# The first recurrence of a fused block, computed two heads at a time

## The reference, cut to what matters

```python
# q, k, v: [heads=4, tokens=512, 64];  g = cumsum(log_sigmoid(f_pre)), i_pre: [heads, tokens]
k = k * 64 ** -0.5
dlog = where(s <= t, g[t] - g[s] + i_pre[s], -1e30)     # exponent of the weight of token s at token t
m_t  = running maximum of dlog over s
w    = exp(dlog - m_t) * (q[t] . k[s])
h[t] = sum_s w * v[s] / max(|sum_s w|, exp(-m_t))
```

## Time and profile before

| | us |
|---|---|
| median of three executions | 2343.0 |
| lowest and highest of the three | 2341.86, 2346.74 |
| the profiled execution, its own time | 2341.32 |
| span of the profiled execution | 2339.5 |
| PE busy in that span | 2204.8 |

### The profile page before, as it was taken

One profiled execution on the slowest core, in us unless ns is written; L12 is line 12 of the kernel. 1 busy time (PEld: TensorE's weight loads), 2 busy tenths in 40 slices (PEclk: granted clock), 3 DMA queues, 4 the chain that ended last, 5 costly groups with the idle time before them and its releaser, 6 DMA issues.

```text
span 2339.5 us, 27011 instructions
## 1 busy us (share of the span) xinstructions
PE 2204.8 (94%) x9972; PEld 1726.2 (74%) x9972; DVE 1051.6 (45%) x1543; ACT 850.3 (36%) x1262; POOL 815.0 (35%) x343
## 2 busy tenths in 40 slices
PE   7888999879999998898899999999999988999999
PEld 5765467658888875564678888878878866888887
DVE  5555565566553434447533212235652575322121
ACT  5423353542222233445443323343432433433231
POOL 3322123324444452220244444443324323444443
PEclk9988999989999999999999999999999999999999
DMA  4212113113332242110223222322212212232233
GB/s 147 72 47 71 37 51 103 55 47 102 121 107 92 98 144 81 46 64 1 64 90 99 91 98 99 98 98 72 77 67 90 68 59 72 90 99 93 96 99 99
DMA packets 54966, 193.35 MB, mean 83 GB/s; under 512 B 6096, under 2 KB 6352, under 8 KB 54480
## 3 DMA queue, kind: packets, MB, share of 16 engines
q1 hardware_dynamic: 50400, 181.58, 23.8%
q10 hardware_dynamic: 4464, 10.36, 1.4%
HBM read 189.82 MB, written 2.10 MB: 82 GB/s over the span
## 4 chain that ended last, share of the span: by engine, by line
PE 72%; issue 14%; DVE 9%; POOL 3%; ACT 2%; DMA 0%; POOLq 0%; SPq 0%; DVEq 0%; ACTq 0%
PE gemm_ps L498 21%; PE gemm_ps L500 21%; PE gemm_ps L499 21%; POOL wl L467 3%; PE out_ps L885 2%; DVE tmp L1620 1%; DVE arena L1989 1%; DVE tmp L1996 1%; PE turn_ps L693 1%; DVE xl L1620 1%; PE score_ps L684 1%; PE out_ps L703 1%; DVE x L1642 1%; PE score_ps L877 1%; DVE arena L1620 1%
## 5 line engine op out<-in xcount | busy, mean ns | idle before, releaser
L467 POOL TENSOR_TENSOR wl<-raw,wh 128x1024 fp32r<-128x1024 f32 x339 | 814.8, 2405 | 1506.7 <-ACT wh L1114 1506.6
L498 PE MATMUL gemm_ps<-xh,wh 128*128 128x512 f32 x1512 | 611.6, 404 | 45.1 <-DVE xl L1620 26.1
L1114 ACT ACTIVATE wh<-raw 128x1024 fp32r<-128x1024 f32 x339 | 359.0, 1059 | 779.6 <-DMA raw<-w_in 751.2
L500 PE MATMUL gemm_ps<-xh,wl 128*128 128x512 f32 x1512 | 592.7, 392 | 0.0
L499 PE MATMUL gemm_ps<-xl,wh 128*128 128x512 f32 x1512 | 592.4, 392 | 0.0
L499 PE MATMUL gemm_ps<-arena_r,wh 128*128 128x512 f32 (+1 forms) x1124 | 432.1, 384 | 0.0
L498 PEld LDWEIGHTS gemm_ps<-xh,wh 128*128 128x128 f32 x1512 | 286.4, 189 | 126.4 <-issue 46.4
L498 PE MATMUL gemm_ps<-arena_r,wh 128*128 128x512 f32 (+1 forms) x868 | 334.3, 385 | 11.0 <-DVE arena_r L1625 10.1
L499 PEld LDWEIGHTS gemm_ps<-xl,wh 128*128 128x128 f32 x1512 | 286.5, 189 | 65.0 <-issue 7.8
L500 PE MATMUL gemm_ps<-arena_r,wl 128*128 128x512 f32 (+1 forms) x868 | 332.5, 383 | 0.0
L500 PEld LDWEIGHTS gemm_ps<-xh,wl 128*128 128x128 f32 x1512 | 286.0, 189 | 60.7
(11 more groups left out here) (313 smaller groups left out, 2042.9 us busy)
## 6 DMA issues: line engine op xcount, KB each, us to landing
raw<-w_in SPq DMA_DIRECT2D x339, 512.0 KB, 3.3
arena<-na_in ACTq DMA_DIRECT2D x14, 256.0 KB, 2.7
x<-x_in SPq DMA_DIRECT2D x8, 256.0 KB, 6.6
out<-x ACTq DMA_DIRECT2D x8, 256.0 KB, 2.8
arena<-alibi_in ACTq DMA_DIRECT2D x6, 256.0 KB, 3.5
con<-con_in SPq DMA_DIRECT2D x1, 1432.0 KB, 12.1
arena<-moba_in ACTq DMA_DIRECT2D x1, 1024.0 KB, 4.9
arena<-mem_in ACTq DMA_DIRECT2D x1, 1024.0 KB, 4.8
```

The costliest lines, as they stand in the source:

```text
L467: pool.tensor_tensor(wl[:, k, :], raw[:, k, :], wh[:, k, :].bitcast(F32), ALU.subtract).then_inc(unit_split, 1)
L498: pe.matmul(o, wh[:, n % RING, w], h[:, kt, 0:width], start=(kt == 0), stop=False)
L500: last = pe.matmul(o, wl[:, n % RING, w], h[:, kt, 0:width], start=False, stop=(kt == nkt - 1))
L1114: act.activation(wh[:, k % RING, :], raw[:, k % RING, :], ACT.Copy).then_inc(high_split, 1)
```

## The change

Only the first recurrence, what surrounds it and the constant `tri` change.

- The unit of work is a key tile j of a pair of heads (p = 0: heads 0 and 1; p = 1: heads 2 and 3), so k = 4p + j runs from 0 to 7. `scores(k)` issues two matmuls, one in rows 0 to 63 and one in rows 64 to 127, into the two banks of `score_ps` or, for odd k, of `gemm_ps`. `outputs(k)` issues the two weighted sums (columns 0 to 63 and 64 to 127) and the two sums of weights (4 columns each, into partitions 0 to 3 and 32 to 35). `scores(k + 2)` follows on `outputs(k)`.
- The exponent: `limits(h)` goes to a place of its own for each head (`limit_ps`). DVE only handles the diagonal 128x128 pieces, adding `tri`, now 0 or -1e30 (`diagonal_limits`). ACT reads the other pieces straight from the bank and the diagonal ones from SBUF, with the key's column as its bias (`exponents`: three plus four instructions). The minimum with zero and the multiplication by the triangle are gone. DVE multiplies the scores into the same place (`gated_scores`).
- The limits, diagonal pieces and exponentials of heads 0 and 1 move into `hgrn()`: PE's two `limits` stand ahead of the last weighted sums, and ACT's 14 exponentials ahead of the copies of `hgrn`'s result. The values are turned into `gemm_ps`, behind `scores(0)`. `limits(3)` writes bank 1 of `out_ps` and so waits for `recurrence_copied`.
- ACT's sigmoids now come after all exponentials; at the end there are two absolute values of four rows instead of one, and one more maximum on DVE.

The diff, cut to this:

```diff
-    at("tri", P)[:] = i[None, :] >= i[:, None]
+    at("tri", P)[:] = np.where(i[None, :] >= i[:, None], 0.0, NEG)
...
+            def limits(h):
+                pe.matmul(limit_ps[h], con[:, CCOL["row"] + h * P:CCOL["row"] + (h + 1) * P],
+                          gate_a, start=True, stop=True).then_inc(bound_ready, 1)
+
             def mlstm():
+                def scores(k):
+                    p, j = divmod(k, T)
+                    for s in range(2):
+                        r = slice(s * HD, (s + 1) * HD)
+                        m = pe.matmul((score_ps, gemm_ps)[k % 2][:, s, j * P:N],
+                                      proj1[r, M_K + p, j * P:(j + 1) * P], proj1[r, M_Q + p, j * P:N],
+                                      start=True, stop=True)
+                    m.then_inc(scores_ready, 1)
+
+                def outputs(k):
+                    p, j = divmod(k, T)
+                    take(weights_ready)
+                    for s in range(2):
+                        pe.matmul(out_ps[s * HD:(s + 1) * HD, p, j * P:N],
+                                  values1[:, j, (2 * p + s) * HD:(2 * p + s + 1) * HD], gated_scores(2 * p + s, j),
+                                  start=(j == 0), stop=(j == T - 1))
+                    for s in range(2):
+                        h = 2 * p + s
+                        m = pe.matmul(turn_ps[32 * s:32 * s + 4, 1, j * P:N],
+                                      con[:, CCOL["col"] + 4 - h:CCOL["col"] + 8 - h], gated_scores(h, j),
+                                      start=(k == 0), stop=(k == 2 * T - 1), skip_group_check=True)
+                    return m
...
+                for k in range(2 * T):
+                    m = outputs(k)
+                    if k + 2 < 2 * T:
+                        scores(k + 2)
+                    if k == T:
+                        turn_attended(0)
+                m.then_inc(weights_used, 1)
...
+            def exponents(h):
+                take(bound_used)
+                col = [small[:, 32 + 4 * j + h:33 + 4 * j + h] for j in range(T)]
+                for j in range(T - 1):
+                    m = act.activation(gated_scores(h, j)[:, P:], limit_ps[h][:, (j + 1) * P:N], ACT.Exp, bias=col[j])
+                m.then_inc(limits_read, 1)
+                for j in range(T):
+                    d = gated_scores(h, j)[:, 0:P]
+                    m = act.activation(d, d, ACT.Exp, bias=col[j])
+                m.then_inc(gate_fun, 1)
...
+            def diagonal_limits(h):
+                take(bound_ready)
+                for j in range(T):
+                    t = slice(j * P, (j + 1) * P)
+                    m = dve.tensor_tensor(gated_scores(h, j)[:, 0:P], limit_ps[h][:, t], c_("tri", P), ALU.add)
+                done(m, bound_used)
+
             def mlstm():
                 r = slice(0, 4)
...
+                for k in range(2 * T):
+                    p, j = divmod(k, T)
+                    if j == 0:
+                        take(gate_fun, 2)
+                    take(scores_ready)
+                    for s in range(2):
+                        w = gated_scores(2 * p + s, j)
+                        done(dve.tensor_tensor(w, (score_ps, gemm_ps)[k % 2][:, s, j * P:N], w, ALU.mult),
+                             weights_ready if s else dve_step)
+                    if k < 2:
+                        diagonal_limits(2 + k)
```

More of the change, by code:

```diff
@@ L739, in turn_attended @@
                 m.then_inc(turned_v, 1)
+            def limits(h):
+                pe.matmul(limit_ps[h], con[:, CCOL["row"] + h * P:CCOL["row"] + (h + 1) * P],
+                          gate_a, start=True, stop=True).then_inc(bound_ready, 1)
             def mlstm():
-                pe.wait_ge(bias_added, len(FIRST_BLOCKS) + 6)
-                turn_values([proj1[:, M_V, :], proj1[:, M_V + 1, :]])
-                take(gate_rows)
-                def limits(h):
-                    pe.matmul(turn_ps[:, 0, :], con[:, CCOL["row"] + h * P:CCOL["row"] + (h + 1) * P],
-                              gate_a, start=True, stop=True).then_inc(bound_ready, 1)
@@ L750, in mlstm @@
-                limits(0)
-                take(recurrence_copied)
-                for h in range(4):
-                    w = weights[h % 2]
-                    r = slice((h % 2) * HD, (h % 2 + 1) * HD)
-                    take(bound_used)
-                    if h < 3:
-                        limits(h + 1)
-                    for j in range(T + 2):
-                        if j == 1 and h == 3:
-                            turn_attended(0)
-                        if j < T:
-                            if h > 0 or j >= 2:
-                                take(scores_used)
-                            pe.matmul(score_ps[:, j % 2, j * P:N], proj1[r, M_K + h // 2, j * P:(j + 1) * P],
-                                      proj1[r, M_Q + h // 2, j * P:N], start=True, stop=True).then_inc(scores_ready, 1)
-                        if j >= 2:
-                            k = j - 2
-                            take(weights_ready)
-                            weighted(h, w, k, start=(k == 0), stop=(k == T - 1))
-                            m = pe.matmul(turn_ps[0:4, 1, k * P:N], con[:, CCOL["col"] + 4 - h:CCOL["col"] + 8 - h],
-                                          w[:, k * N + k * P:(k + 1) * N], start=(h == 0 and k == 0),
-                                          stop=(h == 3 and k == T - 1), skip_group_check=True)
-                    m.then_inc(weights_used, 1)
@@ L774, in mlstm @@
-                take(scores_used, 2)
+                def scores(k):
[6 more added lines that the diff above has]
+                    m.then_inc(scores_ready, 1)
@@ new lines, in mlstm @@
+                pe.wait_ge(bias_added, len(FIRST_BLOCKS) + 6)
+                scores(0)
+                pe.wait_ge(emptied, later_unit(FILL_START + 2 * len(FILL_LEVELS)))
+                for i in range(2):
+                    for t in range(T):
+                        m = pe.transpose(gemm_ps[:, i, t * P:(t + 1) * P], proj1[:, M_V + i, t * P:(t + 1) * P], ident)
+                    m.then_inc(turned_v, 1)
+                pe.wait_ge(limits_read, 1)
+                limits(2)
+                take(recurrence_copied)
@@ L775, in mlstm @@
+                limits(3)
+                take(copied_v, 2)
+                scores(1)
+                for k in range(2 * T):
[5 more added lines that the diff above has]
+                m.then_inc(weights_used, 1)
                 take(copied_v)
@@ L864, in hgrn @@
                         far(0)
+                    else:
+                        take(gate_rows)
+                        limits(0)
+                        limits(1)
                     take(scores_used, 2)
@@ L1826, in limits @@
-                def limits(h):
-                    take(bound_ready)
-                    for j in range(T):
-                        m = dve.tensor_scalar(bound(h, j), turn_ps[:, 0, j * P:N],
-                                              small[:, 32 + 4 * j + h:33 + 4 * j + h], 0.0, ALU.add, ALU.min)
-                    done(m, bound_used)
-                limits(0)
-                for h in range(4):
-                    if h < 3:
-                        limits(h + 1)
-                    take(gate_fun)
-                    if h >= 2:
-                        take(weights_used)
-                    w = weights[h % 2]
-                    for j in range(T):
-                        take(scores_ready)
-                        done(dve.tensor_tensor(w[:, j * N + j * P:(j + 1) * N], score_ps[:, j % 2, j * P:N],
-                                               bound(h, j), ALU.mult), scores_used)
-                        d = w[:, j * N + j * P:j * N + (j + 1) * P]
-                        done(dve.tensor_tensor(d, d, c_("tri", P), ALU.mult), weights_ready)
```

49 lines of the change are left out of this document (25 added, 24 removed).

## The result

| | before | after |
|---|---|---|
| median, us (executions) | 2344.04 (4) | 2315.41 (4) |
| lowest, highest | 2341.86, 2346.74 | 2314.01, 2316.78 |
| profiled execution, span | 2341.32, 2339.5 | 2315.41, 2313.6 |

The ratio is 0.988 (95% interval 0.9868 to 0.9891): 28.6 us faster where 25.3 was forecast, and a time 2.3 under the forecast one. A second comparison later gave 2314.63 against 2344.41, ratio 0.9872 (0.9856 to 0.9889).

A forecast was written before the change was run, and what follows sets the result against it. PE was taken to bound the kernel; the stage ending at 239.7 (223.5 + 16.2) instead of 265.13 saves 25.4 us, less 0.1 behind it: 25.3, giving 2317.7 us, range 2312 to 2326.

The forecast's parts named there:

- What bounds the kernel: PE bounds the whole kernel; the recurrence, 47.3 us without a single unit, is all that the change can shorten.
- A: Stretch from hgrn's last scores to the recurrence's first weighted sums; the forecast has those start at 223.5.
- B: Stretch from the recurrence's first weighted sums to moba's first scores; forecast at 16.2 us.
- Pairs: In the recurrence, two heads' products side by side cost about one, plus 0.5 us for 16 column pairs.
- The first rival: In the recurrence, sums of weights don't pair: + 5.3 us, 2323.0; chance 0.14.
- The third rival: In the recurrence, no pair overlaps and second heads cost in full: + 15.4 us, 2333; chance 0.06.
- C: Stretch from moba's first scores to the second bias products; the longer tail was forecast to cost 0.1 us.
- The start of the pairs: First weighted sums of the recurrence at 223.5, between 223.2 if ACT decides and 225.3 if PE does.
- The second rival: PE starts the pairs late at the low clock: 2319.5 to 2322.5 us; chance 0.16.
- the fourth: The low clock stays through the recurrence or into moba, slower than before: 2358 with 40 us at that level; chance 0.02.
- Behind the stage: After the recurrence, one more absolute value (0.5) and maximum (0.7) show as 0.1 us; nothing else moves.
- The coincidence of DVE and POOL: In moba's first items, DVE's multiplications beside POOL's instruction: up to 1.9 us gained or lost, taken as nothing.

The follow-up runs named there:

- the sums of weights in turn: Changed kernel, but both heads' sums of weights go to the same four partitions, without the second absolute value and extra maximum; 2326.78 us.
- longer tail: Kernel before plus one more absolute value on ACT and one more maximum on DVE behind the recurrence; 2341.65 us against 2344.36, ratio 0.9991.
- two products: Kernel before plus two unused 128x512 products on PE ahead of hgrn's last weighted sums; 2345.0 us, one execution.
- exponent alone: Kernel before, same order, one head at a time, with only the exponent changed and a tiny memset replacing the triangle multiplication; 2344.47 us against 2344.36, ratio 1.000.
- limits behind: Changed kernel, but the limits of heads 0 and 1 stand behind hgrn's last weighted sums instead of ahead; 2319.84 us.
- nothing paired: Changed kernel, but scores, weighted sums and sums of weights of both heads share the same rows or columns; 2332.46 us.

## Why the prediction was right, and where its sizes were off

**What bounds the kernel: right.** 27.6 of the 29.3 us lie where PE had no unit to run (A and B), and microseconds off PE's row came off the span.

**Pairs: right, and cheaper than taken.** B was forecast at 16.2 and is 15.98. Weighted sums and sums of weights of a pair of heads take 5.31 (220.91 to 228.34, less the 2.12 of the scores in between), one head's took 5.27: 0.04 for eight column pairs, 0.08 for all sixteen. I had put 0.5. The Trainium skill's rule on weight loads that share their row groups ("TensorE: Matmul & The Clock Gate", Part 3: Packing small matmuls) gave an estimated 0.9, and the trace does not bear that out: in every pair of L763 and L768 the second head's matmul starts 6 to 8 ns behind the first's, although both use all 128 rows. A table in that section of the Trainium skill, in which column tiles come out within some 5 ns of row tiles, does fit.

**The first rival, sums of weights in turn: did not happen.** It was priced at 5.3 and costs 4.1 (the sums of weights in turn). The price used a whole step of 1.01 for the second product; behind one of the same form it is 0.85. The third rival, nothing pairs, was off in the same way: 15.4 forecast, 11.8 measured in A and B. 24 second products at 0.16 less each are 3.8. That its 2333 almost met the 2332.46 measured is chance: of the 17.05 us over the changed kernel 1.7 come from C, where the short tail is back, and 3.6 from later in the program.

**The start of the pairs: the term that was mis-sized most.** Forecast 223.5; measured 220.91 in a profile that reached `hgrn`'s last scores 0.64 earlier, so 1.95 too late. By its steps, ACT and DVE:

```profile
210.88 1.48 DVE L1961 COPY_PREDICATED y_all<-con,score_ps 128x512 f32<-128x512 uint32 x2 [1.32 <-PE score_ps L874]
212.40 1.80 DVE L1861 TENSOR_TENSOR arena<-turn_ps,con 128x128 f32<-128x128 f32 x8
...
213.38 1.20 ACT L1318 ACTIVATE arena<-turn_ps,small 128x384 f32<-128x384 f32 x3 [4.93 <-DVE arena L1861]
...
217.87 1.09 ACT L1429 ACTIVATE arena<-out_ps 128x512 f32<-128x512 f32 x2
218.82 1.11 ACT L1202 ACTIVATE arena<-gemm_ps 128x512 f32<-128x512 f32 x2
```

- I had the first limits end at 214.1 because a product takes 1.97 at the low clock. The clock was 1.00, and the limits were there before DVE was free. DVE's masked copies ended at 212.36, or 213.0 on the other profile's time, instead of 213.66, since `hgrn`'s last scores took 1.16 and not the 1.83 of the earlier trace rows; and four additions took 0.9, not 1.2: exponentials from 213.38, or 214.02 on the other profile's time, instead of 215.2. That is 1.2 of the 1.95.
- Two heads' exponentials took 4.49, not 4.9: 0.4. So the copies of `hgrn`'s result, which I wanted to see near 220, started at 217.87, or 218.5 on that time.
- The rest, 0.3, is where I went from ACT's 223.2 toward PE's 225.3. ACT decided alone; of its copies it was `hgrn`'s result that PE waited for (1.07 at 219.01), while the values were there in time.

**The clock.** The forecast leaned on the clock coming back by 218, and it was 1.00 all through. The second rival (low clock at the start) and the fourth (it stays low, slower) did not come about. Of its cause the runs show half. These rows of the profile of before stand where it fell:

```profile
223.40 1.24 PE L747 MATMUL turn_ps<-arena,con 128*128 128x512 f32 x2 [2.21 <-DVE arena L1829]
224.57 4.21 PE L764 MATMUL score_ps<-arena 64*128 64x512 f32 x6
```

All kernels of the old order that were profiled (before, longer tail, two products, exponent alone) fell to 0.50 after PE's waits of 1.14 and 2.2 to 2.5 between 216 and 224, and so did the one of the new order whose wait was 2.92; those with 1.08 or less there stayed at 1.00 in the stage. It doesn't hold of every pair of waits: behind those of 1.12 and 1.01 in moba's first items the products took 3.36 and 3.18 in two profiles (sums in turn, exponent alone) and 1.98 in three.

The other half is open. The dip at 210 to 217 was there in the profiles of before and of the longer tail and in none of the other ten, though PE has the same waits up to there in two of them (limits behind, exponent alone). Why it was there isn't settled. By its own rows it made 2.5 us of the 7.15 of A: 1.8 in the weighted sums (4.18 against 2.37) and 0.7 in the last scores (1.83 against 1.16). Part of this came back, as the low stretch in the first head was shorter than in the two kernels without the dip: over A and B the kernel with two products, which has no such dip, is 0.9 below the profile of before (53.94 against 54.87), or 1.1 without what its products cost. That much of the 27.6 us of A and B is the one profile's bad luck and not the change.

**Behind the stage: a mechanism that was named, and taken at nothing.** The 0.1 for the longer tail is there (PE waits 0.17 at 243.22). The coincidence of DVE and POOL was bounded at 1.9 both ways. It came out as 1.7 of gain, and the longer-tail experiment shows that it could have been worked out: DVE had 1.09 of slack and ACT's chain to POOL had none, so that of the added 1.2 POOL's instruction moved by 1.19 and DVE's by 0.14.

The sum: 25.4 forecast for A and B, 27.60 measured (1.95 from the start of the pairs, 0.22 from the pairs); a loss of 0.1 forecast for C, a gain of 1.71 measured. Of the 29.3 us, 11.8 are overlap in the array: 4.1 sums of weights, 2.6 and 0.65 scores, and, by subtraction, 4.4 weighted sums. In B a further 9.3 went without any overlap, by the rows of before and of nothing paired: the two waits for DVE of 1.12, two limits out of PE's row (2.1), score products that moved ahead of the first weighted sums (2.0), changes of form (2.0) and the low clock in the first head (1.1). In A 6.5 went without overlap. The early limits with what hangs on them are worth 4.65 there and the dip at 212 is 2.5 by its rows; the two were taken from different kernels, and add up to a little more than the 6.5.

The low clock can be summed by itself too. In the profile of before it cost the 2.5 of the dip, 1.7 in the first head's three score products (4.13 from start to start, where the second head's take 2.4) and 1.1 behind them: some 5.3 us of A and B, which the changed kernel doesn't have. So a part of what the order and the early limits brought came through the clock: the longest wait of PE left here is 1.07, behind which it stayed at 1.00, while in the kernel with the limits behind it was at 0.50 after the wait of 2.92.

## What to carry to other kernels

Where PE has nothing but small products, count them by step and not by size: two heads in different rows or columns cost one, and a product behind one of its own form 0.16 us less than behind another. Look at the first wait of such a stage as closely as at its steady part, since moving a few instructions of PE ahead of it was worth 4.65 us here, 1.1 of it by the clock, and a cheaper operation alone (the exponent) nothing that the whole time shows. And where two engines disturb each other in the trace, work out which of them the change delays by more; whether they still meet follows from their slack.

## What the runs showed of the hardware that I had not expected

- **DVE behind POOL.** DVE's two 128x128 multiplications by a column (SBUF to SBUF) take 0.61 us, but 2.57 when they start while POOL's 128x1024 subtraction runs: in the kernel before they end at 276.02, 0.40 after POOL's end; with the sums of weights in turn they start at 250.01, end at 252.59, and POOL's ends at 252.18. In both it is the first of the two that takes 2.25, and it ends 0.08 after POOL's; the second takes its usual 0.3. Of the 80 multiplications of L1775 in the kernel before, this is the only one that starts inside an instruction of POOL, and no other takes more than 0.49. So DVE stood still until POOL was all but done. The Trainium skill ("SBUF — State Buffer", Who interferes with whom) says that such an operation can enter a mode that needs the port pair shared with POOL, and then blocks for the whole of the other's instruction. The trace agrees with the blocking (2.25 us beside POOL's 2.35); that the mode was entered no run shows.
- **A longer tail made the next stretch shorter**, by 1.84 us in the kernel before (12.40 to 10.56).
- **Column pairs are as good as free**: 0.04 us for eight, 64 or 4 columns wide and in turn with row pairs, against 0.85 for a second product of 512 columns that shares its columns.
